# Filler products at the stage ends of a hybrid decoder layer, and four pieces of work moved across stage borders

## The reference

```
h = rmsnorm(x) * (1 + sc1) + sh1                     # sc1, sh1, ... from silu(c) @ ada_w + ada_b
q, kv, gates, qkv_dilated, merge = split(h @ w_in)
o_nsa = g0 * compressed + g1 * selected + g2 * windowed attention    # 8 heads, gates = sigmoid
o_dil = three dilated attention groups, joined by their softmax denominators
merged = sigmoid(m0) * (o_nsa @ w_up_nsa) + sigmoid(m1) * (o_dil @ w_up_dil)
x = x + g1 * (merged @ w_o)
h = rmsnorm(x) * (1 + sc2) + sh2
x = x + g2 * MoE(h)          # top-1 of 4 groups, top-2 of its 8 experts, each (silu(h@w1)*(h@w3))@w2
out = rmsnorm(x)
```

## Time and profile before

| | us |
|---|---|
| median of 3 runs | 1801.01 (1800.58 to 1801.04) |
| profiled execution, its own time | 1804.73 |
| its span in the trace | 1802.9 |
| PE busy | 1680.9 (93%) |
| PEld busy | 1133.4 (63%) |
| DVE, ACT, POOL busy | 606.0, 415.9, 178.8 |
| mean granted clock of TensorE | 0.969 |

### The profile page before, as it was taken

One profiled execution on the slowest core, in us unless ns is written; L12 is line 12 of the kernel. 1 busy time (PEld: TensorE's weight loads), 2 busy tenths in 40 slices (PEclk: granted clock), 3 DMA queues, 4 the chain that ended last, 5 costly groups with the idle time before them and its releaser, 6 DMA issues. The chain is left out here.

```text
span 1802.9 us, 37075 instructions
## 1 busy us (share of the span) xinstructions
PE 1680.9 (93%) x16013; PEld 1133.4 (63%) x16013; DVE 606.0 (34%) x1568; ACT 415.9 (23%) x933; POOL 178.8 (10%) x220
## 2 busy tenths in 40 slices
PE   5999999998999999899999989969999999998892
PEld 3444446897787777644444445547787778777772
DVE  3533331002667666666554322261011101110003
ACT  4000000003666656410100011112121222112122
POOL 1205000000111110000000000001111111111110
PEclk9899999998999999999999999978999999999996
DMA  9874224311101107424533082149999999999985
GB/s 335 249 220 120 71 83 131 76 59 41 43 2 43 31 26 218 132 71 125 156 104 102 18 321 87 53 176 377 344 395 401 397 392 400 402 390 395 391 308 206
DMA packets 155456, 355.74 MB, mean 197 GB/s; under 512 B 15519, under 2 KB 94999, under 8 KB 138875
## 3 DMA queue, kind: packets, MB, share of 16 engines
q1 hardware_dynamic: 128112, 303.14, 45.2%
q0 software_dynamic: 13456, 27.93, 5.8%
q10 hardware_dynamic: 13724, 22.27, 3.6%
HBM read 321.58 MB, written 47.13 MB: 205 GB/s over the span
## 5 line engine op out<-in xcount | busy, mean ns | idle before, releaser
L2413 PE MATMUL psum<-sb_m_xT,sb_m_ring 128*64 128x64 f32 (+1 forms) x4096 | 174.3, 243 | 4.2 <-issue 4.1
L2413 PEld LDWEIGHTS psum<-sb_m_xT,sb_m_ring 128*64 128x64 f32 x4096 | 167.4, 137 | 16.5 <-issue 14.7
L2332 DVE TENSOR_TENSOR sb_m_hT<-psum,sb_m_sg 128x128 f32<-128x128 f32 (+1 forms) x64 | 22.0, 346 | 338.6 <-ACT sb_m_sg L2194 338.5
L2413 PE MATMUL psum<-sb_m_xT,sb_front 128*64 128x64 f32 (+1 forms) x2560 | 108.9, 242 | 13.6 <-issue 6.6
L2194 ACT ACTIVATE sb_m_sg<-psum 128x128 f32<-128x128 f32 (+1 forms) x64 | 20.5, 321 | 424.9 <-PE psum L2413 424.9
L2413 PEld LDWEIGHTS psum<-sb_m_xT,sb_front 128*64 128x64 f32 x2560 | 103.3, 139 | 22.1 <-issue 21.0
L1703 PE MATMUL psum<-sb_w_o_sb,sb_mT 128*128 128x512 f32 x256 | 115.7, 606 | 0.0
L717 PE MATMUL psum<-sb_vD,sb_room 128*128 128x512 f32 x240 | 104.6, 592 | 0.0
L2181 ACT ACTIVATE sb_m_xT<-psum,sb_rowmod 128x64 f32<-128x64 f32 (+1 forms) x256 | 84.8, 437 | 40.2 <-PE psum L2401 40.2
L974 ACT ACTIVATE sb_d_probs<-sb_d_probs,sb_d_nmax 128x640 f32<-128x640 f32 (+7 forms) x128 | 92.9, 735 | 1.5 <-DVE sb_d_nmax L1014 1.0
L749 PE MATMUL psum<-sb_b_wvd,sb_rows 128*128 128x256 f32 x384 | 88.9, 393 | 0.0
(11 more groups left out here) (339 smaller groups left out, 2357.0 us busy)
## 6 DMA issues: line engine op xcount, KB each, us to landing
sb_m_ring<-in_exp_w_dram SPq DMA_DIRECT2D x48, 2048.0 KB, 29.0
sb_front<-in_exp_w_dram SPq DMA_DIRECT2D x30, 2048.0 KB, 29.0
sb_rows<-in_exp_w_dram SPq DMA_DIRECT2D x18, 2048.0 KB, 27.5
sb_g_ada<-in_ada_w_dram SPq DMA_DIRECT2D x16, 1024.0 KB, 5.3
d_qk<-sb_n_b_sel ACTq DMA_DIRECT2D x20, 512.0 KB, 3.2
sb_front<-in_w_in_dram SPq DMA_DIRECT2D x16, 512.0 KB, 5.2
sb_front<-d_qk SPq DMA_DIRECT2D x15, 512.0 KB, 6.9
sb_n_b_sel<-in_w_in_dram SPq DMA_DIRECT2D x10, 512.0 KB, 8.6
```

The costliest lines, as they stand in the source:

```text
L2413: mm = pe.matmul(k.psum[part, c // 2, col:col + w], views[which][:, kk, c * P + CAPS * h:c * P + CAPS * (h + 1)], x[:, kk, 0:w], start=(kk ...
```

## The change

A helper `idle_products` issues n matmuls of 512 columns, the identity times constants, into a PSUM bank that nobody reads. It is called at the end of the lists of TensorE in stage a (3), b (1), d (2), e (1), in the last part of stage h (3, 1 and 1), and in stage m after the product that spreads the expert rows, L2386 (8). Beside this:

- the sigmoid of the gates moves from the end of stage b to behind the copy of job 16;
- the stores of the last set of stage e count on a semaphore that lives on; the barrier no longer waits for them, SP waits at the start of stage g instead. Their source buffer is allocated first, so that stage g's early writes miss it;
- the last `gated` (block 7, second half) and its add leave stage g and become the first two instructions of DVE in stage h; GpSimd's last add goes away. TensorE waits for the first before it turns x into the same banks, and for the second before tile 4;
- `hidden(0)`, the two multiplies that make `hT` of block 0, moves ahead of DVE's work on the overflow slots.

```diff
+def idle_products(pe, k, bank, n):
+    for _ in range(n):
+        pe.matmul(k.psum[:, bank, :], k.ident, k.const[:, 0:BANK], start=True, stop=True)
...
             mod_cols(3)
+            pe.wait_ge(s_evd, evacs[-1][0])
+            pe.wait_ge(s_eva, evacs[-1][1])
+            idle_products(pe, k, 4, 3)
...
-            act.wait_ge(s_va, len(vjobs) // 2)
-            act.wait_ge(s_vd, len(vjobs) // 2)
-            act.activation(gates[:, :, :], graw[:, :, :], ACT.Sigmoid).then_inc(s_va, 1)
+                if n == OUT_AT + 2:
+                    act.wait_ge(s_va, NT // 2)
+                    act.wait_ge(s_vd, NT // 2)
+                    act.activation(gates[:, :, :], graw[:, :, :], ACT.Sigmoid).then_inc(s_gates, 1)
...
+            idle_products(pe, k, 3, 1)
...
+            pe.wait_ge(s_biased, before[NS])
+            idle_products(pe, k, 0, 2)
...
+                stored = k.s_dil if n == SETS - 1 else s_store
...
-            sp.wait_ge(s_store, 16 * 2 * SETS)
+            sp.wait_ge(s_store, 16 * 2 * (SETS - 1))
...
+            pe.wait_ge(s_biased, 4 * NS)
+            idle_products(pe, k, 0, 1)
...
+            sp.wait_ge(k.s_dil, 32)
             for g in range(DIL_G):
                 sp.dma_start(dl[:, g].rearrange("p t h c -> p t (h c)"),
...
-                if c >= 1:
+                if 1 <= c < KD:
                     gated(c - 1, 1)
...
-            for u in range(U):
+            for u in range(U - 1):
...
+                if t == NT // 2:
+                    pe.wait_ge(s_last, 2)
                 out(t, 0, range(KD))
                 if t == 1:
+                    pe.wait_ge(s_last, 1)
                     pe.wait_ge(s_prep, 2)
...
             route(NT - 1)
+            pe.wait_ge(s_mul, 2 * NT - 2)
+            idle_products(pe, k, 1, 3)
             pe.wait_ge(s_hot, 2)
...
             mm.then_inc(s_rank, 1)
+            idle_products(pe, k, 1, 1)
             pe.wait_ge(s_hotr, 1)
...
             pe.wait_ge(s_be_ps, 1)
+            idle_products(pe, k, 1, 1)
...
+            dve.tensor_tensor(last, k.psum[:, 4:6, :], last, ALU.mult).then_inc(s_last, 1)
+            dve.wait_ge(s_last, 1)
+            dve.tensor_tensor(mT[:, KD - 1, BANK:], last[:, 0, :], last[:, 1, :], ALU.add).then_inc(s_last, 1)
+            dve.wait_ge(s_last, 2)
             dve.wait_ge(k.s_router, 64)
...
+            hidden(0)
             dve.wait_ge(s_slots, 2)
...
             for b in range(NE):
-                for half in range(2):
-                    dve.wait_ge(s_silu, 2 * b + half + 1)
...
+                if b >= 1:
+                    hidden(b)
...
                       start=True, stop=True).then_inc(s_perexp, 1)
+            idle_products(pe, k, 6, 8)
```

More of the change, by code:

```diff
@@ L538, in stage_projections @@
             "zero", "blocks", "hidden", "gelu", "out_ps", "out", "tables"))
+        s_gates = k.sem("b_gates")
         w_in = k.w_in[0].rearrange("(k p) n -> p k n", p=P)
@@ L1051, in stage_dilated @@
         SETS = DIL_G * DIL_H // 2
+        last_stage = sb("last_stage", [P, NT, 2, DH + 2])
         q2 = sb("q2", [P, S])
@@ L1057, in stage_dilated @@
         keys, bias = ([held[n % HELD][j] for n in range(SETS)] for j in range(2))
-        stage = [sb(f"stage{n}", [P, NT, 2, DH + 2]) for n in range(SETS)]
+        stage = [sb(f"stage{n}", [P, NT, 2, DH + 2]) for n in range(SETS - 1)] + [last_stage]
         probs = [[sb(f"probs{i}{x}", [P, BANK]) for x in range(2)] for i in range(3)]
@@ L1123, in _ @@
                         sp.dma_start(rows.rearrange("(t p) h c -> p t (h c)", p=P)[:, four, :], st[:, four, :]
-                                     ).then_inc(s_store, 16)
+                                     ).then_inc(stored, 16)
                     elif g == 1:
                         sp.dma_start(rows.rearrange("(b j r) h c -> b j r (h c)", b=2, r=4)[half], st[:, half::2, :]
-                                     ).then_inc(s_store, 16)
+                                     ).then_inc(stored, 16)
                     else:
                         sp.dma_start(rows.rearrange("(m w) h c -> m w (h c)", w=8)[:, four, :], st[:, four, :]
-                                     ).then_inc(s_store, 16)
-            sp.wait_ge(s_store, 16 * 2 * SETS)
+                                     ).then_inc(stored, 16)
+            sp.wait_ge(s_store, 16 * 2 * (SETS - 1))
         @block.tensor
@@ L1632, in stage_out @@
         small = room[:, 6 * D:]
+        last = room[:, (NT + 4) * BANK:(NT + 8) * BANK].rearrange("p (g h t) -> p g h t", g=2, h=2)[:, :, 1, :]
+        s_last = k.sem("h_last_gated")
         at = [0]
@@ L2308, in _, with hidden @@
             dve.tensor_copy(w_small[:, :], k.psum[:, 4, UNITS + 2 * NBIG:2 * UNITS]).then_inc(s_idx, 1)
+            def hidden(b):
+                for half in range(2):
+                    dve.wait_ge(s_silu, 2 * b + half + 1)
+                    if half == 0 and b >= 1:
+                        dve.wait_ge(s_y, b)
+                    up = k.psum[:, half, 0:4 * width[b]].rearrange("p (c g n) -> p c g n", c=2, g=2)[:, :, 1, :]
+                    tt(hT[:, 2 * half:2 * half + 2, 0:width[b]], up, sg[half][:, :, 0:width[b]], ALU.mult
+                       ).then_inc(s_hid, 1)
+            hidden(0)
             dve.wait_ge(s_slots, 2)
@@ L2326, in _ @@
             for b in range(NE):
-                for half in range(2):
-                    dve.wait_ge(s_silu, 2 * b + half + 1)
-                    if half == 0 and b >= 1:
-                        dve.wait_ge(s_y, b)
-                    up = k.psum[:, half, 0:4 * width[b]].rearrange("p (c g n) -> p c g n", c=2, g=2)[:, :, 1, :]
-                    tt(hT[:, 2 * half:2 * half + 2, 0:width[b]], up, sg[half][:, :, 0:width[b]], ALU.mult
-                       ).then_inc(s_hid, 1)
+                if b >= 1:
+                    hidden(b)
                 dve.wait_ge(s_y, b + 1)
@@ L2491, in build @@
         s_wo = k.sem("w_o")
-        k.s_router, k.s_set0 = k.sem("router"), k.sem("first_set")
+        k.s_router, k.s_set0, k.s_dil = k.sem("router"), k.sem("first_set"), k.sem("dilated_stored")
         k.s_first = [k.sem(f"first_expert{i}") for i in range(AHEAD)]
```

## The result

| | before | changed |
|---|---|---|
| runs | 4, median 1800.80 us (1797.02 to 1801.04) | 4, median 1780.72 us (1778.93 to 1781.83) |
| ratio | | 0.9897, 95% interval 0.9879 to 0.9915 |
| profiled execution, its span | 1804.73, 1802.9 | 1781.83, 1780.0 |
| mean granted clock | 0.969 | 0.981 |

The forecast was 1780 us. To see whether its terms were right too, I cut both profiles at the first TensorE instruction of each stage and at three more points: stage b's third product (the first that reads `vD`), the turns of the joined output in stage g, and the end of the last down product. Lengths in us, with the forecast's terms beside them.

A forecast was written before the change was run, and what follows sets the result against it. TensorE was busy 93% of the span, idle mostly at stage borders with a cold clock behind, the expert stage paced by weights; 0 - 3.6 - 1.3 - 3.6 - 5.8 - 0.4 - 6.2 = -20.9 from 1801.0 gave 1780 us, range 1774 to 1789.

The forecast's parts named there:

- Stage a, 0.0: Border a to b: three fillers start stage b up to 2.3 us late, warm products return it; bounds +1.0 and -0.9.
- Barriers: Stage starts earlier by the border's work alone: b to d -1.3, d to e no cost, e to g -3.1, g to h -2.9.
- Stage d's clock, -2.3: Start of stage d: if the clock stays up, cold work shrinks by 4.1 at most, taken as -2.3; lower bound 0.
- Stage e's clock, -1.3: Start of stage e: the clock returns at most 2.7 us; softmax steps between halve that, to -1.3.
- Stage g, -0.5 beyond its start: Stage g up to the joined output: limited by the stores' landing and VectorE's chain; whole border -3.6, bounds -2.4 and -4.5.
- Stage h, -3.3: Stage h: dense products behind the border run warm, -2.9; fillers and a shorter DVE chain at its end, -0.4.
- Expert stage, -6.2: Expert stage beyond its earlier start: block 0 ends 10.1 us earlier, DMA idle time allows 6.8 at most, 6.2 taken.
- rival D: Expert stage: fillers run cold, first turn waits 5 us, DMA idle time stays, term about -1; 1785 us, chance 0.07.
- Its signs of being wrong: Clock 0.50 behind a border with fillers; waits for weights not growing; a stage starting over 1 us after its last real work.
- A: At the borders the clock falls all the same, clock terms go, expert term some 4.7: sum -12.0, 1789 us, chance 0.14.
- B: Expert stage: the whole 10 us arrive, which needs a stage paced by TensorE; 1776 us, chance 0.08.
- C: Slower than before: gathers and added outputs slow the expert stage's weight stream, below 378 GB/s from 395; chance 0.03.

The follow-up runs named there:

- the reverse move: The changed kernel with the last gated multiply and its add put back in stage g: 1785.31 us, ratio 0.9916.
- light loads: Half of the bytes of each expert matrix reloaded from the eleventh on, in the kernel before (1791.40 us, 0.9943) and the changed kernel (1761.80 us, 0.9773).
- the second set of fillers: Changed kernel without stage a's fillers, with two inside stage d's steps and, in stage m, one ahead of the diagonal's wait and nine behind: 1778.21 us, ratio 0.9869.

## Why the prediction was right, and where it was not

**The time** came out at 1780.72 against 1780. The sum of the profile's differences is -22.9 us, of which 2.2 are the chance of stage a's own pace; the rest, -20.7, stands against the sum of -20.9. That they agree so closely is luck: stage a came out 0.6 us worse than forecast and stage d 1.6, the joined output 1.2 better and the expert stage 0.7.

**Stage a, 0.0: right in sum.** Behind TensorE's end the changed kernel needed 13.57 us to the third product, 13.00 before: +0.6, inside the bounds. The fillers ran cold, held the barrier, and the warm products gave it back. But the bounds (+1.0 and -0.9) took for granted that the clock is 0.50 when the fillers begin. In four other profiles it was 1.00, and the distance 11.0 us, 2.0 less than before. The price of a filler was also low: 5.25 us for six records make 1.75 us for a product, not 1.71, and three of them took 5.47 us cold (1.82 each) and 2.82 warm (0.94 each).

**Barriers: right everywhere.** b to d -1.3 for -1.3, d to e 0, e to g -3.0 for -3.1, g to h -3.0 for -2.9.

**Stage d's clock, -2.3: wrong in its cause.** It measured -0.7, and -0.7 without any filler as well; over the eight profiles with the changed stage d it was between -1.6 and +0.6. One warm filler ahead of the border, with 0.88 us of gap behind it, does not keep the clock through the first steps, where TensorE waits for VectorE (0.49 us of work in the first us, 0.55 in the second); it fell at 429.8. The forecast sized the cold time rightly (two fillers inside the steps return 2.7 from 240.81), and expected it from the wrong place.

**Stage e's clock, -1.3: right**, -1.2 (half of it is there without fillers too).

**Stage g, -0.5 beyond its start: mis-sized, it was -1.7.** The wait for the landing was right (1.61 for 1.7). But I had VectorE's chain behind it fixed in length. Before, this chain had itself waited 0.27 and 0.54 us for gate products of TensorE that came late behind the cold start; it shrank from 19.15 us (765.17 to 784.32) to 18.16 (758.18 to 776.34). And TensorE took its result 0.2 us behind its end instead of 1.7, so the slack was used up as forecast. The whole border came to -4.7, just past my bound of -4.5.

**Stage h, -3.3: right**, in both parts (the reverse move cost 3.0 and 2.6).

**Expert stage, -6.2: right in size, by other shares.** Block 0's down product ended 9.35 us earlier behind the stage's start (forecast 10.1). The turn came at 13.8 us, not at 12.6, since the fillers ran at 0.50 until 1194.4: a part of rival D, which cost 1.2 us. The idle time of the DMA engines between the loads was the limit as forecast: the share rose from 0.66 to 0.99, and 6.9 us arrived. The loss is seen in the blocks behind: from the end of block 0's down product to the end of the last they took 518.6 us before and 521.1 after (521.3 in the second profile), 2.5 us more, where the forecast had 3.9 (10.1 less 6.2). The table of waits does not measure it: the waits for weights and those without a releaser in the expert stage make 19.2 us before, and 21.1 and 14.0 in two profiles of the changed kernel. With light loads the same blocks took 508.4 and 504.2 us, and the waits 5.2 and 1.9, so the limit is real, and most of those waits are for the loads.

**Fillers or moves.** The prediction gave each border a barrier part and a clock part and took the clock for the fillers' doing; by that division the moves alone were to bring 11 us. They bring 17.8 of the 21.0, since the clock stays up at the borders of g and h without a filler.

**Its signs of being wrong.** Two of the three came up, although the time was right. The clock fell to 0.50 behind borders with fillers, in stage d and in the expert stage, and stage b started 3.4 us after its last real work (48.06 to 51.44). The third, that the waits for weights don't grow, the table of waits can't decide.

**The rivals.** A (the clock falls all the same) was true in stage d and for the expert stage's fillers only. B (the full 10 us) is refuted by the light loads, C by a stream of 393 GB/s after, against 395 before.

Stage g begins with 32 transposes, and its clock was 1.00 through them (744.4 to 747.6), with a filler ahead and without one. The rule that I had set beside rival A, that transposes do not engage the full clock (the Trainium skill, "TensorE: Matmul & The Clock Gate", Part 4: PE-mode transpose), would have let it fall here; these traces do not bear it out, for a clock that was full before.

## What to carry to other kernels

First take away what ends a stage behind TensorE: here gaps of up to 2.28 us ahead of dense work left the clock at 1.00, gaps of 3.6 us and more did not, and most of what the fillers seemed to do was done by the moved work. A filler pays where a real wait of TensorE follows a border, in the first dependent steps, and costs where it runs cold and is the last to arrive at the barrier or delays work whose input has landed. One profile does not tell which of the two a filler does: those of stage a did either, from one profile to the next. And in a stage that a stream paces, count what idle time of the stream the change removes: that is the gain, whatever TensorE gains.

## What the runs showed of the hardware

The clock also falls in the middle of a stage, and is then low where TensorE is busy throughout. In stage g, among dense products of 512 columns, the profile after has 3.4 us at 0.50 (busy time by stretch):

```profile
897.00:898.00 1.00, 1.00 (x4) 0.64 (x4) 0.76 (x3) 0.00 (x0) 0.72 (x1) 0.72 0.00 0
898.00:899.00 1.00, 1.00 (x2) 0.34 (x1) 0.93 (x3) 0.00 (x0) 0.00 (x0) 0.50 0.00 0
899.00:900.00 1.00, 1.00 (x2) 0.34 (x1) 0.93 (x3) 0.00 (x0) 0.00 (x0) 0.50 0.00 0
900.00:901.00 1.00, 1.00 (x3) 0.39 (x2) 0.96 (x2) 0.00 (x0) 0.00 (x0) 0.58 0.00 0
901.00:902.00 1.00, 1.00 (x4) 0.52 (x3) 0.48 (x1) 0.00 (x0) 0.00 (x0) 1.00 0.00 0
```

It costs 1.7 us: the piece from the joined output's turns to the border takes 262.1 us with such a fall, as in both profiles of the changed kernel, and 260.4 without it, as in those of the second set of fillers and of no fillers in the expert stage, which do not differ from it in this piece. The 265.1 before has one too (0.96 over 940 to 980 us).

Ahead of the fall stand twelve records of one column, with a wait for VectorE between them (timeline):

```profile
894.88 0.95 PE L1581 MATMUL psum<-sb_const,sb_g_acc 128*128 128x1 f32 x8
896.59 0.58 PE L1581 MATMUL psum<-sb_const,sb_g_acc 128*128 128x1 f32 x4 [0.76 <-DVE sb_mod L1427]
```

Each of the fourteen profiles has this group twice in stage g. Ten have one fall between the start of stage g's dense products and its end, and each of these ten begins between 0.1 us ahead of the end of such a group and 0.9 us behind it; four have none. In the expert stage the fall at 1185.4 of the second set of fillers also stands behind records of one column. So what precedes the fall is known here; why it comes behind some of these groups and not behind others (10 of 28) no run shows, and none was run without them.
